# Head norms of a hybrid decoder step: a sum of squares in f32, or in two rounded parts

## The reference

```python
def _rmsnorm(x, g):
    xf = x.astype(jnp.float32)
    y = xf * lax.rsqrt(jnp.mean(xf * xf, axis=-1, keepdims=True) + EPS)
    return (y * g.astype(jnp.float32)).astype(x.dtype)

    o_h = _rmsnorm(o_h, hgrn_norm).astype(h.dtype) * jax.nn.silu(zg).reshape(B, L, HGRN_HEADS, HGRN_DV)
    o_g = _rmsnorm(o_g, gla_norm).astype(h.dtype) * jax.nn.silu(gr).reshape(B, L, GLA_HEADS, GLA_DV)
```

## Time and profile before

| | us |
|---|---|
| median of 3 runs | 1680.25 |
| lowest and highest | 1679.14 to 1681.83 |
| the profiled execution | 1679.9 |
| its span | 1678.1 |
| PE busy in it | 1661.7 |
| DVE, ACT, POOL busy in it | 1096.3, 807.8, 204.8 |
| the head stage | about 265 to 637 |

### The profile page before, as it was taken

The page is one execution under the profiler, slowest core; times in us unless marked ns, Lnnn a source line. Parts: engine busy times, 40 slices in busy tenths (PEclk is TensorE's granted clock), DMA queues, the critical chain, the costliest instruction groups (busy, mean ns, idle before and its releaser), DMA issues.

```text
span 1678.1 us, 36823 instructions
## 1 busy us (share of the span) xinstructions
PE 1661.7 (99%) x13668; PEld 1656.2 (99%) x13668; DVE 1096.3 (65%) x1824; ACT 807.8 (48%) x1102; POOL 204.8 (12%) x196
## 2 busy tenths in 40 slices
PE   7999999999999999999999999999999999999999
PEld 7999999999999999999999999999999999999999
DVE  7548557998988886665697445554455445555775
ACT  7565435556465455543565334443344334443452
POOL 3100001211212110015330000000000000025200
PEclk9999999999999999999999999999999999999999
DMA  9455766575665566775555555555555655555564
GB/s 265 151 190 169 229 203 194 168 217 185 185 225 191 179 208 207 233 265 175 174 177 176 193 182 174 177 192 182 173 179 176 199 176 175 175 196 179 167 191 147
DMA packets 162546, 318.67 MB, mean 190 GB/s; under 512 B 11700, under 2 KB 96436, under 8 KB 162500
## 3 DMA queue, kind: packets, MB, share of 16 engines
q1 hardware_dynamic: 160196, 315.91, 58.8%
q10 hardware_dynamic: 2304, 2.16, 0.4%
HBM read 299.94 MB, written 18.09 MB: 190 GB/s over the span
## 4 chain that ended last, share of the span: by engine, by line
PE 97%; DMA 1%; DVE 1%; issue 1%; ACT 0%; SPq 0%; DVEq 0%; ACTq 0%
PE bank L310 27%; PE bank L311 27%; PE bank L312 27%; PE bank L328 3%; PE bank L329 3%; PE bank L330 3%; PE bank L600 2%; PE bank L613 1%; DMA lev<-m_spill 1%; PE bank L589 1%; PE bank L631 0%; PE bank L645 0%; PE bank L639 0%; PE bank L611 0%; DMA raw<-in_stream 0%
## 5 line engine op out<-in xcount | busy, mean ns | idle before, releaser
L293 ACT CAST whi<-raw 128x1024 fp32r<-128x1024 f32 x534 | 547.8, 1048 | 461.0 <-PE bank L312 358.5
L298 DVE TENSOR_TENSOR wlo<-raw,whi 128x1024 fp32r<-128x1024 f32 x534 | 647.9, 1244 | 139.5 <-ACT whi L293 138.2
L310 PE MATMUL bank<-a_hi,whi 128*128 128x264 f32 x2576 | 737.1, 286 | 0.3 <-DVE a_lo L1348 0.3
L311 PE MATMUL bank<-a_lo,whi 128*128 128x264 f32 x2576 | 729.9, 283 | 0.0
L312 PE MATMUL bank<-a_hi,wlo 128*128 128x264 f32 x2576 | 729.7, 283 | 0.0
L310 PEld LDWEIGHTS bank<-a_hi,whi 128*128 128x128 f32 x2576 | 485.4, 188 | 1.0 <-issue 0.9
L311 PEld LDWEIGHTS bank<-a_lo,whi 128*128 128x128 f32 x2576 | 485.6, 189 | 0.1
L312 PEld LDWEIGHTS bank<-a_hi,wlo 128*128 128x128 f32 x2576 | 483.1, 188 | 0.0
L310 PE MATMUL bank<-b_hi,whi 128*128 128x264 f32 x1280 | 363.2, 284 | 0.6 <-issue 0.6
L311 PE MATMUL bank<-b_lo,whi 128*128 128x264 f32 x1280 | 362.6, 283 | 0.0
L312 PE MATMUL bank<-b_hi,wlo 128*128 128x264 f32 x1280 | 362.4, 283 | 0.0
(11 more groups left out here) (178 smaller groups left out, 1544.2 us busy)
## 6 DMA issues: line engine op xcount, KB each, us to landing
raw<-in_stream SPq DMA_DIRECT2D x534, 512.0 KB, 4.4
m_spill<-stage SPq DMA_DIRECT2D x32, 132.0 KB, 5.2
lev<-m_spill SPq DMA_DIRECT2D x16, 264.0 KB, 5.2
S<-in_state_hgrn SPq DMA_DIRECT2D x16, 256.0 KB, 5.4
out_new_hgrn_sample<-S SPq DMA_DIRECT2D x16, 256.0 KB, 4.6
S<-in_state_gla SPq DMA_DIRECT2D x8, 512.0 KB, 7.9
out_new_gla_sample<-S SPq DMA_DIRECT2D x8, 512.0 KB, 5.6
room<-in_x SPq DMA_DIRECT2D x7, 528.0 KB, 7.7
```

Of the source, the lines that this page charges most:

```text
L293: act.copy(whi[:, s, :], raw[:, s, :]).then_inc(hi_ready, 1)
L298: dve.tensor_tensor(wlo[:, s, :], raw[:, s, :], whi[:, s, :].bitcast(F32), ALU.subtract).then_inc(lo_ready, 1)
L310: pe.matmul(out, whi[:, s, w], hi[:, k0 + k, :], start=start and k == 0, stop=False)
L311: pe.matmul(out, whi[:, s, w], lo[:, k0 + k, :], start=False, stop=False)
```

## The change

ACT squares each bank twice: once to `sq` as before and once to `sq_hi`, rounded to fp32r. DVE makes the low part `sq_lo = sq - sq_hi` (in the memory of `sq`). PE sums both with rounded matmuls, first the high parts, then, behind a wait for a new semaphore `sq_parts`, the low parts. In a GLA head the sum moves from the middle of slab 7 to its end, and `state` stays in the middle; on DVE the subtraction stands ahead of the first levels in an HGRN head and behind them in a GLA head.

```diff
+    with nc.sbuf_tensor("sq_lo", [P, 2, TOK], F32R) as sq_lo:
+        pass
     sq = sb("sq", [P, 2, TOK])
+    sq_hi = sb("sq_hi", [P, 2, TOK], F32R)
...
         def head_norm(H, D):
             pe.wait_ge(h_sem["sq_ready"], now(H))
             for d in range(D):
-                mm = pe.matmul(DG[:, 0:TOK], ones[:], sq[:, d, :], start=d == 0, stop=d == D - 1)
+                pe.matmul(DG[:, 0:TOK], ones[:].bitcast(F32R), sq_hi[:, d, :], start=d == 0, stop=False)
+            pe.wait_ge(h_sem["sq_parts"], now(H))
+            for d in range(D):
+                mm = pe.matmul(DG[:, 0:TOK], ones[:].bitcast(F32R), sq_lo[:, d, :], start=False, stop=d == D - 1)
             mm.then_inc(h_sem["ss_done"], 1)
...
             def norm_and_state():
+                if D == 1:
+                    head_norm(H, D)
+                state(H, D)
+
+            slab(7, midway=norm_and_state)
+            if D == 2:
                 head_norm(H, D)
-                state(H, D)
-
-            slab(7, midway=norm_and_state)
...
             act.wait_ge(h_sem["pv_done"], now(H))
             act.wait_ge(h_sem["ss_done"], before(H))
             for d in range(D):
-                sqd = act.activation(sq[:, d, :], O[d][:, 0:TOK], ACT.Square)
+                act.activation(sq[:, d, :], O[d][:, 0:TOK], ACT.Square)
+                sqd = act.activation(sq_hi[:, d, :], O[d][:, 0:TOK], ACT.Square)
             sqd.then_inc(h_sem["sq_ready"], 1)
             slab(8)
...
             slab(7)
             m_tile(2)
+
+            def square_parts():
+
+                dve.wait_ge(h_sem["sq_ready"], now(H))
+                dve.wait_ge(h_sem["ss_done"], before(H))
+                dve.tensor_tensor(sq_lo[:, 0:D, :], sq[:, 0:D, :], sq_hi[:, 0:D, :].bitcast(F32), ALU.subtract)\
+                   .then_inc(h_sem["sq_parts"], 1)
+
+            if D == 1:
+                square_parts()
             if more:
                 dve.wait_ge(h_sem["cum_ready"], now(H + 1))
                 level_half(0)
+            if D == 2:
+                square_parts()
             slab(8)
```

More of the change, by code:

```diff
@@ L209, in build @@
                 "ln_rs", "rs_ready", "o_hi_done", "s_out_ready", "sg_abs", "sg_exp", "sg_ln", "sg_sigma"],
-        "dve": ["s_parts_ready", "lev_sub", "lev_ready", "kd_ready", "s_new0", "s_new1", "masked", "probs_ready", "sg_ls",
+        "dve": ["s_parts_ready", "lev_sub", "lev_ready", "kd_ready", "s_new0", "s_new1", "sq_parts", "masked", "probs_ready", "sg_ls",
                 "sg_ready", "o_scaled", "o_gated", "o_done"],
@@ L674, in norm_and_state @@
             def norm_and_state():
-                head_norm(H, D)
+                if D == 1:
+                    head_norm(H, D)
                 state(H, D)
             slab(7, midway=norm_and_state)
+            if D == 2:
+                head_norm(H, D)
         with pe.Fori(0, HH) as H:
```

## The result

| | before | changed |
|---|---|---|
| median, us (6 runs each) | 1679.47 | 1685.28 |
| lowest and highest | 1678.29 to 1681.83 | 1683.65 to 1689.36 |
| profiled execution | 1679.9 | 1683.65 |
| its span | 1678.1 | 1681.9 |

A forecast was written before the change was run, and what follows sets the result against it. A closed loop Square, ACT, DVE, prob_v, Square was taken to bound the head stage, PE waiting on it; 1.68 + 0.22 + 0.26 + 2.07 + 0.13 = 4.4 us gave a median of 1684.6 us, range 1680.4 to 1687.0.

The forecast's parts named there:

- ACT's square: Second Square of each bank on ACT, on the loop before the slab cast: 0.28 us, 0.56 in a GLA head.
- PE's saving: Rounded sums give PE back 0.20 us for each of 16 products, 3.3 us in all, off the loop.
- DVE at nothing: DVE's added subtraction booked at nothing, hidden in its wait for ACT's slab cast; uncovered, 0.34 us per HGRN head.
- PE's new wait for the low part: HGRN heads: low part ready at 342.41, asked for at 342.64, so no wait, with 0.2 us to spare.
- The wait at the Ln of the GLA sum: GLA sum moved behind slab 7 ends later than ACT's Ln needs it: 0.13 us on the loop, bounds 0 and 0.3.
- Heads 0 to 6: HGRN heads, prob_v to prob_v: six rounds, each longer by 0.28 us, 1.68 us in all.
- Head 6 to 7: Round to head 7's prob_v: 0.28 us less the 0.06 by which PE was last, 0.22 us.
- to head 8's scores: From head 7's prob_v to the scores of head 8: 0.28 us less up to 0.04, 0.26 us.
- heads 8 to 11: GLA heads, scores to scores: three rounds of 0.56 + 0.13 = 0.69 us, 2.07 us in all.
- The end: After the heads, where PE stands until the last spill tile is drained: drain at 636.48 instead of 636.35, 0.13 us.
- The forecast's inner ends: Forecast's own range: 1683.4 us (zero wait at L921, smaller squares) to 1686.5 us (0.39 us for each square).
- Rival A: PE is the bound and its gain arrives in each head: -3.3 us, 1677.0 us; chance 0.10.

## Why the prediction was right, and where its sum was short

The direction, the engine and the mechanism were right: the measured 1685.28 lies 0.7 us above the 1684.6 forecast and inside the range, though against the medians of this comparison the change is 5.8 us (4.4 to 7.7) and the sum was 4.4. That the median came out so near 1684.6 is in part luck: the forecast started from a median of the kernel before of 1680.25 us, and the comparison's was 1679.47. Term by term:

- *ACT's square, 0.28 us.* Measured 0.27 in an HGRN head and 0.56 for two, by the kernel with the squares alone. The trace's start-to-start time was the right price. The Trainium skill (ScalarE: Activation LUTs, Rules for kernel authors) has about 0.3 us for an ACTIVATE plus 0.83 ns an element, an estimate of 0.52 us for one square. It states this for a bias given as a pointer operand, which the Square's call doesn't pass, so the figure was the wrong one to put beside this square; the runs don't agree with it.
- *PE's saving, worth nothing.* With the saving alone the rounds moved by 0.02 us or less.
- *DVE at nothing.* Right; 1.07 us were to be left of its cover, 1.13 were.
- *PE's new wait for the low part, none.* Right in the changed kernel (0.12 us between high and low product); it appears as soon as ACT's cast goes first, and in the GLA heads with the sum midway.
- *The wait at the Ln of the GLA sum, 0.13 us.* It was 0.15 in the trace and 0.16 by undoing it.
- *Heads 0 to 6, 1.68 us: the mis-sized term.* It measured 2.14 us. The step booked 0.28 us a round, for ACT alone, and took the gapless DVE stretch as fixed. The additions to `pairs` in it grew from 2.42 to 2.51 us. That POOL's copies lengthen them is shown, for holding the copies back gave 0.26 us a round; that they do so by 0.09 us more because they start 0.5 us earlier against the additions is read from the traces and wasn't isolated.
- *Head 6 to 7, 0.22; to head 8's scores, 0.26; heads 8 to 11, 2.07.* These measured 0.19, 0.23 and 2.23.
- *The end, 0.13.* PE resumes 0.14 us later against head 11's scores, as forecast. Behind it PE has a new wait of 0.6 us between two slabs, up to 652.7 us, and one of 0.3 us, up to 733.2 us in the kernel before, is not there. The 0.4 us by which the part behind the heads was longer in the profiled execution are within its spread, so whether the change causes them is open, as is the last microsecond between the 4.8 us of the head stage and the medians' 5.8.

Of the signs, one was placed wrongly: PE's idle time in a GLA head was expected at the scores as 1.6 us; it is 1.14 us at `outer`, behind POOL's `k_diag`, and 0.48 at the scores, since `outer` is the first place where the late loop is met. Another was too large: PE's busy time fell by 1.9 us where some 3 were forecast. And the prediction books nothing for POOL, whose copies turned out to lie on the loop and, at `turn_s`, at its edge. The forecast's inner ends were not worked out to the end either: a wait of zero at L931 takes 0.4 us off the sum, and squares of 0.39 us add 1.5, so they give 1684.2 and 1686.1 where 1683.4 and 1686.5 stand. Rival A would have led to the wrong sign: 5.2 us taken from PE alone left the time where it was. The Trainium skill (Perfetto Trace Analysis, Identifying the Most-Contended Engine) has the rule behind A, the engine of highest occupancy first; here that rule doesn't hold. The same page's Optimization Strategy also tells to find what blocks the engine in its gaps, and the runs bear that out. Its remark that the most contended engine changes between stretches doesn't fit this case, although the prediction took the 0.59 us as agreeing with it: PE has the highest occupancy in both head stages, and what limits both is a loop through several engines.

## What to carry to other kernels

When an engine reads 99% busy, look for the place where another engine's last result and its first use keep the same distance from one iteration to the next. Such a distance says that the busy engine may be waiting there, and an experiment that takes work from it alone says whether it is. If it is, an instruction on a half-idle engine can cost its full start-to-start time, as the square did here. Before work is moved from the busy engine to the others, first empty their way (here, a cast put into a wait was worth 0.9 us a GLA head), and expect the next wait right behind. The price of producing a result late depends on how early its consumer is: the moved sum cost 0.16 us a head, and 1.1 us once the cast was out of the way.

## What the runs showed of the hardware

A POOL copy of 128x264 f32 that falls on a DVE addition of 128x128 f32 lengthens it from 0.29 to 0.38 or 0.47 us, and with the copies out of the way the seven additions take 2.25 in place of 2.51 us. A POOL copy of 24 columns lasted 2.1 to 3.9 us in some kernels and 0.2 to 0.9 us in others, beside gapless DVE work in both; what decides between the two wasn't isolated. A rounded matmul of 264 columns that has to wait for its operand is followed by the next start after 0.22 us, where one that doesn't wait is followed after 0.12 (341.17 - 340.95 with the cast first and the sum midway, 372.64 - 372.52 in the changed kernel).
